# Where the gated row tiles of the expert layer are made: VectorE alone, or GpSimd's distances and one VectorE instruction

## The reference, cut to what matters

```python
s = einsum('thpc,hpnc->thpn', q, sub_keys)       # 8 heads, two halves of 128 keys
s1, i1 = top_k(s[:, :, 0], 16); s2, i2 = top_k(s[:, :, 1], 16)
cand = s1[..., :, None] + s2[..., None, :]
best, ci = top_k(cand, 16)                       # 16 of 256 pairs for each head
e1, e2 = i1[ci // 16], i2[ci % 16]               # row and column of the expert
expert = e1 * 128 + e2; gate = softmax(best)     # 8 * 16 = 128 slots for each token
act = gelu(h @ u_tab[expert]) * gate
out = act @ v_tab[expert]
```

## Time and profile before

| what | value |
|---|---|
| median of 3 runs | 3676.75 us (3674.76 to 3676.95) |
| the profiled execution, its own time | 3679.92 us |
| its span, first to last instruction | 3677.8 us |
| mean granted TensorE clock | 0.982 of full speed |
| TensorE busy | 3496.8 us (95%) |
| VectorE busy | 2487.5 us (68%) |
| ScalarE busy | 1599.1 us (43%) |
| GpSimd busy | 36.3 us (1%) |
| gate stage, first `hot_col` to last `hot_row` | 114.69 us |

### The profile page before, as it was taken

The page is one execution under the profiler, slowest core; times in us unless marked ns, Lnnn a source line. Parts: engine busy times, 40 slices in busy tenths (PEclk is TensorE's granted clock), DMA queues, the critical chain, the costliest instruction groups (busy, mean ns, idle before and its releaser), DMA issues.

```text
span 3677.8 us, 70211 instructions
## 1 busy us (share of the span) xinstructions
PE 3496.8 (95%) x24822; PEld 3002.3 (82%) x24822; DVE 2487.5 (68%) x4311; ACT 1599.1 (43%) x2507; POOL 36.3 (1%) x49
## 2 busy tenths in 40 slices
PE   8999899999999899888888988999999999999998
PEld 6888788888888777777777876888888888888887
DVE  6766686767677777666655699556565656565666
ACT  5445444444444455433334214535353535353543
POOL 0000000000000000000000001000000000000000
PEclk9999999999999999999999999999999999999999
DMA  5545455555555444300034434565656555565554
GB/s 196 169 143 167 137 191 178 179 177 189 170 194 171 155 138 141 123 9 9 20 99 160 143 128 177 181 212 180 213 184 212 187 204 197 191 207 190 201 193 144
DMA packets 165705, 593.81 MB, mean 161 GB/s; under 512 B 18432, under 2 KB 26752, under 8 KB 164288
## 3 DMA queue, kind: packets, MB, share of 16 engines
q1 hardware_dynamic: 159600, 559.12, 45.6%
q0 software_dynamic: 5968, 32.77, 2.3%
HBM read 572.68 MB, written 18.87 MB: 161 GB/s over the span
## 4 chain that ended last, share of the span: by engine, by line
PE 85%; DVE 10%; ACT 2%; issue 1%; DMA 1%; DVEq 0%; SPq 0%; ACTq 0%; POOLq 0%
PE bank L564 50%; PE bank L565 25%; PE bank L897 5%; DVE hot_row L2682 1%; DVE hot_col L2677 1%; DVE w_lo L1827 1%; PE bank L585 1%; DVE proj L2387 1%; ACT w_hi L1252 1%; PE bank L868 0%; PE bank L842 0%; PE bank L1218 0%; PE bank L908 0%; DMA gates<-g_stage 0%; DVE acc L1893 0%
## 5 line engine op out<-in xcount | busy, mean ns | idle before, releaser
L564 PE MATMUL bank<-h_two,w_hi 128*128 128x512 f32 x5360 | 1904.0, 400 | 53.3 <-DVE h_two L1885 23.1
L565 PE MATMUL bank<-h_two,w_lo 128*128 128x256 f32 x5360 | 1504.6, 281 | 0.0
L1827 DVE TENSOR_TENSOR w_lo<-raw,w_hi 128x1024 fp32r<-128x1024 f32 (+1 forms) x1054 | 1227.8, 1184 | 237.1 <-ACT w_hi L1252 235.5
L1252 ACT ACTIVATE w_hi<-raw 128x1024 fp32r<-128x1024 f32 (+1 forms) x1054 | 1046.0, 1024 | 538.8 <-PE bank L565 490.3
L564 PEld LDWEIGHTS bank<-h_two,w_hi 128*128 128x128 f32 x5360 | 1010.9, 189 | 305.8 <-issue 42.4
L565 PEld LDWEIGHTS bank<-h_two,w_lo 128*128 128x128 f32 x5360 | 1017.0, 190 | 1.1 <-issue 0.7
L564 PE MATMUL bank<-p_two,w_hi 128*128 128x512 f32 x1792 | 631.1, 395 | 2.4 <-DVE acc L1852 1.2
L565 PE MATMUL bank<-p_two,w_lo 128*128 128x256 f32 x1792 | 506.8, 283 | 0.0
L564 PEld LDWEIGHTS bank<-p_two,w_hi 128*128 128x128 f32 x1792 | 336.6, 188 | 83.9 <-DVE p_two L2696 5.6
L565 PEld LDWEIGHTS bank<-p_two,w_lo 128*128 128x128 f32 x1792 | 337.5, 188 | 0.0
L1848 DVE TENSOR_TENSOR acc<-acc,bank 128x256 f32 x192 | 80.8, 421 | 370.1 <-PE bank L565 370.1
(11 more groups left out here) (365 smaller groups left out, 3084.4 us busy)
## 6 DMA issues: line engine op xcount, KB each, us to landing
raw<-in_u_tab SPq DMA_DIRECT2D x256, 512.0 KB, 4.1
raw<-in_v_tab SPq DMA_DIRECT2D x256, 512.0 KB, 4.5
raw<-in_w_up SPq DMA_DIRECT2D x176, 512.0 KB, 4.3
raw<-in_w_in SPq DMA_DIRECT2D x174, 512.0 KB, 3.8
raw<-in_w_out SPq DMA_DIRECT2D x64, 512.0 KB, 4.2
raw<-in_w_down SPq DMA_DIRECT2D x64, 512.0 KB, 3.6
raw<-in_w_pq SPq DMA_DIRECT2D x32, 512.0 KB, 4.8
gates<-g_stage POOLq DMA_DIRECT2D x16, 896.0 KB, 5.3
```

The source lines that it names most:

```text
L564: nc.tensor.matmul(o[:], wh, pair.rearrange("p a t -> p (a t)"), start=(k == 0), stop=False)
L565: last = nc.tensor.matmul(o[:, T:2 * T], wl, pair[:, 0, :], start=False, stop=(k == nk - 1))
L1252: nc.scalar.activation(w_hi[c % 2][:, at:end], raw[c % 2][:, at:end], ACT.Copy).then_inc(hi_done, 1)
L1827: nc.vector.tensor_tensor(w_lo[c % 2][:, at:end], raw[c % 2][:, at:end], w_hi[c % 2][:, at:end].bitcast(F32), ALU.subtract).then_inc(lo_do ...
```

## The change

GpSimd computes for each step the distance between the numbers 0 to 127 and the slot's row, for four tokens in one instruction, into a new tile `far` (two buffers, on memory that `sub_k` used before). VectorE then makes `hot_row` for four tokens in one instruction: where the distance is zero, the slot's gate, else zero. GpSimd runs up to two steps ahead: its instruction for step n waits until `hot_row` of step n-2 is made. The issue of each store now stands in GpSimd's queue between the distances of steps 4b+5 and 4b+6. VectorE has one wait more in each step (`pool_set`).

```diff
+        far_at = ExitStack()
+        far = [sb(f"far{j}", [P, 4, P], at=far_at) for j in range(2)]
+        far_at.close()
         sub_k = sb("sub_k", [P, 2 * PEER_H, P], at=top_at)
...
+            def distances(n):
+                if n >= 2:
+                    pool.wait_ge(hot_ready, n - 1)
+                nc.gpsimd.tensor_tensor(
+                    far[n % 2][:], count[:, 0:P].unsqueeze(1).to_broadcast([P, 4, P]),
+                    slot_T[:, 0, 4 * n:4 * n + 4].unsqueeze(2).to_broadcast([P, 4, P]), ALU.subtract
+                    ).then_inc(pool_set, 1)
+
+            pool.wait_ge(sub_loaded, 32)
+            pool.wait_ge(turned_copied, 1)
+            for n in range(4):
+                distances(n)
             for b in range(T // 16):
-                pool.wait_ge(gates_copied, 8 * (b + 1))
-                pool.dma_start(gates_d[1:PEER_G, :, 16 * b:16 * b + 16, :].rearrange("g p t e -> p g (t e)"),
-                               g_stage[b % 2][:, 1:PEER_G].rearrange("p g t e -> p g (t e)")
-                               ).then_inc(gates_stored[b % 2], 16)
+                for n in range(4 * b + 4, 4 * b + 8):
+                    if n < T // 4:
+                        distances(n)
+                    if n == 4 * b + 5:
+                        pool.wait_ge(gates_copied, 8 * (b + 1))
+                        pool.dma_start(gates_d[1:PEER_G, :, 16 * b:16 * b + 16, :].rearrange("g p t e -> p g (t e)"),
+                                       g_stage[b % 2][:, 1:PEER_G].rearrange("p g t e -> p g (t e)")
+                                       ).then_inc(gates_stored[b % 2], 16)
...
-                for x in range(4):
-                    t = 4 * n + x
-                    last = nc.vector.tensor_scalar(hot_row[n % 2][:, x, :], count[:, 0:P], slot_T[:, 0, t:t + 1],
-                                                   slot_T[:, 2, t:t + 1], ALU.is_equal, ALU.mult)
-                last.then_inc(hot_ready, 1)
+                dve.wait_ge(pool_set, 2 + n + 1)
+                nc.vector.scalar_tensor_tensor(
+                    hot_row[n % 2][:], far[n % 2][:], 0.0,
+                    slot_T[:, 2, 4 * n:4 * n + 4].unsqueeze(2).to_broadcast([P, 4, P]), ALU.is_equal, ALU.mult
+                    ).then_inc(hot_ready, 1)
```

## The result

The changed kernel takes 3709.43 us (median of 4 runs, 3706.59 to 3711.61), the kernel before 3676.85 us (4 runs). The ratio is 1.0085, with a 95% interval of 1.0072 to 1.0098: 32.6 us slower. The prediction was 3728.5 us, with a range of 3682 to 3765 and 0.81 for slower.

A forecast was written before the change was run, and what follows sets the result against it. VectorE was taken to bound the gate stage. With VectorE and GpSimd alternating at SBUF, 64 x 2.515 = 161.0 us, plus 4.5 and 0.9, made 166.4 against 114.7: 3676.75 + 51.7 = 3728.5 us, range 3682 to 3765.

The forecast's parts named there:

- What bounds the stage: Gate stage: VectorE bounds it at 1.656 us a step, GpSimd is nearly idle, TensorE needs 1.33 us a step.
- VectorE's own work: VectorE in the gate stage: falls to 0.60 + 0.60 = 1.20 us a step, 0.45 less; alone 29 us.
- Turns: VectorE and GpSimd exclude each other at SBUF in the gate stage: +51.7 us, 3705 to 3765 us, chance 0.65.
- The evidence for turns: Old hot_row group stretched from 1.10 to 1.32 us beside store issues, taken as showing both engines wait at SBUF.
- the step of 2.515 us: Gate stage: half a two-step cycle of 2.48 us VectorE, 2.40 us subtracts and handover; 64 steps make 161.0 us.
- the handover: Passing SBUF between VectorE and GpSimd: 0.15 us taken, from semaphore rows giving 0.05 to 0.31 us.
- The store's issue: Store issue in GpSimd's queue, 0.95 us: said to lie under VectorE's turn, adding nothing to the sum.
- The cycle: Gate stage counted in two steps: four VectorE instructions back to back, two subtracts, two handovers; 5.03 us.
- TensorE's clock: TensorE in the first 48 steps: a lower clock could add 19 us; counted as nothing, in full for upper bound.
- The signs: Expected in the changed profile: stretched records, hot_col well over 693 ns, steps of 2.4 to 2.7 us, chain through GpSimd.
- Half turns: Gate stage: only one VectorE instruction meets the subtract, or access is shared; 1.90 us a step, +12.3, 3689 us, chance 0.16.
- The no-meeting case: Gate stage: engines do not meet, GpSimd's queue bounds; four steps 6.35 us, -5.4 us, 3671 us, chance 0.18.

## Why the prediction was right, and where its sizes were off

*What bounds the stage.* Right. VectorE held it, TensorE's 1.33 us is the floor without GpSimd, and the rest of the kernel did not move.

*VectorE's own work.* Right: 0.60 us for the new instruction from start to start, 1.20 a step.

*Turns.* Right, and shown from several sides: the records stretch with the subtract, not with a write-only instruction of nearly the same length, not when VectorE's second operand is in PSUM, and they stretch too when nobody waits for the subtract. This is the rule of the Trainium skill that the prediction cited (SBUF — State Buffer, "Who interferes with whom"); the runs agree with it in reads against second SBUF inputs and in writes left alone. They show 0.85 of the subtract's 1.04 us blocked, and they show the small instructions, with one tensor input, kept out as well.

*The evidence for turns.* The row that the prediction rested them on, beside the page, did not carry them. The stretched `hot_row` of the kernel before is a small instruction beside a store's issue; the new one beside an issue stays at 681 to 686 ns, and a `w_lo` pair beside one stays at 2.35 us. So what an issue does to one form of instruction does not tell what a subtract does to another. The choice of 0.65 for turns was right, and as far as it came from this row it was luck.

*The term that was mis-sized* is the step of 2.515 us in the sum with turns. Measured it is 2.05. Taken apart: VectorE 1.20 instead of 1.24; the subtract 1.04 instead of 1.20 us; and the handover, which the sum has at 0.075 a step to be added, is 0.19 to be taken off, since 0.19 us of a subtract run beside VectorE's instructions. Together 0.04 + 0.16 + 0.265 = 0.465 us, times 64 = 30 us too much. The handover was the worst guess: I took it from waits on semaphores, while VectorE waits here inside its records. The sum has a slip there besides: it names two handovers of 0.15 us in two steps and adds one. With both a step is 2.59 us and the forecast 3733; the steps of 2.37 and 2.81 us among the rivals have both. And their upper ends together, 71 + 10 + 19 = 100 us, give 3777, above the 3765 of the range. Neither would have turned the forecast the other way.

*The store's issue.* Wrong: "lies under VectorE's turn". It costs 0.62 us each, about 10 us in all, and VectorE is kept out over it where it comes ahead of a subtract. The two errors have opposite signs; 51.7 - 30 + 10 = 32, near the measured 32.6, the small terms aside. That the forecast is only 19 us off is in part luck: this term, put at nothing, hides a third of the error of the step.

*The cycle.* I had each engine take two instructions in a row. In a plain step they alternate: `hot_col`, subtract, `hot_row`. The engines' own times in the sum do not depend on it, but the handovers do: there are two in each step and not two in two steps.

*TensorE's clock.* No cost seen, as taken. In the stage the granted clock is 0.91 against 0.93 before: 0.96 in its first 100 us and 0.80 in the last 45, in which VectorE is still shown busy for 43.95.

*The signs.* Steps of 2.4 to 2.7 us and a `hot_col` well over 693 ns in many steps were named, and the chain passing through GpSimd. Plain steps are 2.05 us, 12 of 64 `hot_col` but 44 of 64 `hot_row` are over 1 us, and the chain from 2185 us to the stage's end has no piece on GpSimd: it stays mostly on VectorE, whose records hold the waiting.

*The rivals.* Half turns came out in the kernels with one operand in PSUM, at 3695 and 3697 instead of the 3689 reckoned. The no-meeting case came out as the kernel with both, 6.32 us for four steps against the 6.35 of the prediction, and 3673 against 3671. That the figures agree so well is luck: with the measured subtract of 1.04 us the rival's own way is 6.03, and the way through TensorE that it did not have adds nearly what the subtract saves.

## What to carry to other kernels

Before work goes to an idle GpSimd, look at what each VectorE instruction beside it reads from SBUF: with two tensors, GpSimd's reads are not free time but added to VectorE's, here 0.85 of 1.04 us, and the small instructions with one tensor and two columns paid 0.7 us as well. The cheapest way out is often the operand's place: a small second operand left in PSUM removed the meeting of these two instructions at no cost in VectorE's time (673 to 689 ns). And a helper's queue needs slack ahead of each wait it contains: two more buffers and a later issue made 3673 into 3662 us (ratios 0.9986 and 0.9957).

## What had not been expected of the hardware

A waiting VectorE instruction is shown busy, not idle, so VectorE seemed busy for 99% of the stage though 0.85 us of each 2.05 were waiting; the record's minimum (676 ns) against its median (1521) tells it.

A store's issue by itself left the new instruction alone (681 to 686 ns in the kernel without subtracts), yet issue and following subtract together gave it records of 2.2 to 2.4 us in 6 blocks, in which it had started 0.1 to 0.3 us after the issue. In other blocks a `hot_row` that started at that point was through undisturbed, and the `hot_col` behind it was kept out. It looks as if the queued subtract can have its claim before the issue is over; no run separates that from other causes, so it stays open.
